# Expert weights in nine places, gathered rows turned by VectorE, and the last feed-forward closed by token halves

## What is computed

```python
# experts: 32, two for each token out of one group of 8
hid = jax.nn.silu(xb @ w_gate[e]) * (xb @ w_up[e])   # w_gate, w_up: 1024 x 256
ys = (hid @ w_down[e]) * gate                        # w_down: 256 x 1024
out = segment_sum(ys, slot_tok)                      # back to tokens, two rows each

# the end of the second block
f2 = swiglu(rms_norm(h, ffn2_pre_g), w_gate, w_up, w_down)
h = h + 0.5 * rms_norm(f2, ffn2_post_g)
```

## Time and profile before

| | us |
|---|---|
| median of 3 runs | 2992.62 (2992.49 to 2992.73) |
| the profiled execution, own time | 2994.38 |
| its span, first to last instruction | 2992.6 |
| TensorE busy with matmuls | 2944.8 |
| VectorE (DVE), ScalarE (ACT), GpSimd (POOL) busy | 1288.2, 652.6, 814.6 |

### The profile page before, as it was taken

One profiled execution on the slowest core, in us unless ns is written; L12 is line 12 of the kernel. 1 busy time (PEld: TensorE's weight loads), 2 busy tenths in 40 slices (PEclk: granted clock), 3 DMA queues, 4 the chain that ended last, 5 costly groups with the idle time before them and its releaser, 6 DMA issues.

```text
span 2992.6 us, 31855 instructions
## 1 busy us (share of the span) xinstructions
PE 2944.8 (98%) x12562; PEld 1882.5 (63%) x12562; DVE 1288.2 (43%) x2193; ACT 652.6 (22%) x1082; POOL 814.6 (27%) x621
## 2 busy tenths in 40 slices
PE   9999999999999999999999999999999999999998
PEld 7865464333468754643334588888664445888887
DVE  6734443111446435431223554442573464644442
ACT  2035313111210263231112400001212351300001
POOL 5500022222124010222221144443210102344442
PEclk9999999999999999999999999999999999999999
DMA  5211125999622101249997222222221211222220
GB/s 191 85 71 43 44 90 211 381 385 389 236 72 95 73 29 57 71 159 378 377 374 314 85 85 85 85 99 92 92 77 57 71 43 58 84 85 85 86 98 28
DMA packets 81380, 412.68 MB, mean 138 GB/s; under 512 B 25872, under 2 KB 26256, under 8 KB 34768
## 3 DMA queue, kind: packets, MB, share of 16 engines
q1 hardware_dynamic: 56608, 387.57, 34.1%
q0 software_dynamic: 24624, 23.08, 2.4%
HBM read 513.31 MB, written 31.46 MB: 182 GB/s over the span
## 4 chain that ended last, share of the span: by engine, by line
PE 93%; DVE 4%; ACT 1%; issue 1%; DMA 0%; SPq 0%; POOL 0%; DVEq 0%; ACTq 0%; POOLq 0%
PE PS L1111 38%; PE PS L1045 11%; PE PS L613 8%; PE PS L1067 6%; PE PS L598 4%; PE PS L691 4%; PE PS L571 4%; PE PS L1289 4%; PE PS L1019 1%; PE PS L846 1%; PE PS L530 1%; PE PS L786 1%; PE PS L903 1%; PE PS L912 1%; PE PS L1356 1%; PE PS L518 1%
## 5 line engine op out<-in xcount | busy, mean ns | idle before, releaser
L3105 POOL TENSOR_TENSOR ATT<-ring 128x512 f32<-128x512 f32 (+1 forms) x97 | 126.2, 1301 | 1186.7 <-PE PS L1111 630.8
L1111 PE MATMUL PS<-G,ATT 128*128 128x256 f32 x1344 | 317.8, 379 | 0.0
L1111 PE MATMUL PS<-HT,ring 128*128 128x256 f32 x1376 | 313.8, 379 | 0.8 <-DVE BIG L1518 0.8
L1111 PE MATMUL PS<-G,ring 128*128 128x256 f32 x1216 | 287.6, 379 | 0.0
L1111 PEld LDWEIGHTS PS<-HT,ring 128*128 128x128 f32 x1376 | 261.2, 190 | 39.5 <-issue 2.4
L1111 PEld LDWEIGHTS PS<-G,ATT 128*128 128x128 f32 x1344 | 255.4, 190 | 36.0 <-issue 1.2
L2827 ACT ACTIVATE TMP<-PS 128x256 f32<-128x256 f32 x91 | 35.0, 384 | 1051.7 <-PE PS L1111 934.5
L613 PE MATMUL PS<-HT,ring 128*128 128x512 f32 x576 | 263.3, 600 | 0.0
L1111 PEld LDWEIGHTS PS<-G,ring 128*128 128x128 f32 x1216 | 231.0, 190 | 31.4
L1045 PE MATMUL PS<-ring,G 128*64 128x512 f32 x1024 | 226.9, 595 | 0.6 <-ACT G L2796 0.6
L613 PEld LDWEIGHTS PS<-HT,ring 128*128 128x128 f32 x576 | 104.5, 190 | 127.4 <-issue 120.9
(11 more groups left out here) (385 smaller groups left out, 4375.7 us busy)
## 6 DMA issues: line engine op xcount, KB each, us to landing
ring<-in_stream SPq DMA_DIRECT2D x163, 1024.0 KB
ring<-in_experts_gu SPq DMA_DIRECT2D x128, 1024.0 KB
ring<-in_experts_down SPq DMA_DIRECT2D x64, 1024.0 KB
G<-expert_rows SPq DMA_DIRECT2D x8, 1024.0 KB, 6.9
h_tokens<-G POOLq DMA_DIRECT2D x2, 2048.0 KB, 7.6
XT<-in_xT SPq DMA_DIRECT2D x1, 1024.0 KB, 8.3
G<-in_pT POOLq DMA_DIRECT2D x2, 512.0 KB, 6.3
out_T<-XT SPq DMA_DIRECT2D x2, 512.0 KB, 3.7
```

What stands on the lines that cost most here:

```text
L1111: mm = pe.matmul(product(g, name), x[:, k * P:(k + 1) * P], y[:, k, :], start=first and k == 0 and name in opening, stop=last and k == h - ...
L3105: pool.tensor_tensor(a["S1"], a["A21"], a["A22"], ALU.add)\
```

## The change

**Nine places.** While the experts run, three more regions hold units: two in BIG (tiles 16 to 23) and one in ATT (tiles 7 to 10), and main blocks fill the nine in turn (`PLACE`, `Ring.experts`). SP fills the two in BIG once the attention branches are projected, the one in ATT once the output projection is done, all ahead of the stage. To make room the tail weights take 4 instead of 6 units (`TW`): the down weights land where the first half of gate and up weights lay, so POOL issues them later, after that half is used; the next gate and up weights wait for the down product. Some scratch of the router and of the rotary tables moves within ATT.

**Rows turned by VectorE.** Only blocks 0 to 5 (`FIRST_BLOCKS`) keep `turn_x` and the ACT copy. For blocks 6 to 23, POOL gathers the rows in four pieces, each of 128 rows of 256 values (`gather_squares`, L3131 in the new numbering), so arranged that the 32 x 32 squares that DVE turns in one instruction (`turned_rows`, L2062, 128 x 4 x 8 x 32) land in `XGT` as the products need them. The features are numbered otherwise for it (row p*8 + k of the weights in place of k*128 + p; the weights are laid out so on the host), and `turn_x` reads XG with a stride of eight values (32 bytes). The row numbers of the pieces come from four small products (`quad_tables`), a DVE copy ahead of the stage and one behind `hidden(0)`.

**The end by halves.** The fourth chunk of `ffn(1)` becomes a `halved_chunk` with `half_norm`, and scaling, residual and store go by token halves. In the second half TensorE and ACT add tiles 4 to 7 (`OWN_X` is 4, was 3), with 256 columns each; there are six stores in place of four, half as wide.

The core of the diff:

```diff
@@ constants and places
+PLACES = 9
+SQUARE = 32
+SQUARES = P // SQUARE
+QD = D // SQUARES
+FIRST_BLOCKS = 6
+            def experts(self):
+                order = [(self.place + i) % RING if i < RING else i for i in range(PLACES)]
+                for n in range(6 * PAIRS):
+                    p = order[n % PLACES]
+                    self.fills[p] += 1
+                    yield p, self.fills[p]
-        TW = BIGF[:, 0:12 * D].rearrange("p (s n) -> p s n", s=2)
+        TW = BIGF[:, 0:8 * D].rearrange("p (s n) -> p s n", s=2)
+        PLACE = ([ring[:, i, :] for i in range(RING)] + [BIGF[:, (16 + 4 * i) * S:(20 + 4 * i) * S] for i in range(2)]
+                 + [ATT[:, 7 * S:11 * S]])
-        OWN_X = 3
+        OWN_X = 4
@@ TensorE, expert stage
                     for k in range(KD):
-                        mm = pe.transpose(PSF[:, o + k * P:o + (k + 1) * P],
-                                          XG[:, q % 2, k * P:(k + 1) * P], IDENT)
+                        mm = pe.transpose(PSF[:, o + k * P:o + (k + 1) * P], XG[:, q % 2, k:D:KD], IDENT)
...
-                        return [TW[:, side, j * UNIT:(j + 1) * UNIT] for side in range(2)], []
+                        return [TW[:, side, j % 2 * UNIT:(j % 2 + 1) * UNIT] for side in range(2)], []
...
+                def quad_tables():
+                    pe.wait_ge(Q["tab_ready"], now.next("tab_ready"))
+                    for g in range(SQUARES):
+                        mm = pe.matmul(PS[:, 7, g * NSEQ:(g + 1) * NSEQ], QUAD_LANES[:, g * P:(g + 1) * P], RT["tab"][:, 0:NSEQ],
+                                       start=g == 0, stop=True, skip_group_check=True)
...
                 gate_up(0)
+                quad_tables()
                 gate_up(1)
...
                     turn_hidden(q - 1)
-                    if q + 1 < NSEQ:
+                    if q + 1 < FIRST_BLOCKS:
                         turn_x(q + 1)
@@ DVE, expert stage
+                def turned_rows(q):
+                    v.wait_ge(Q[f"x_gather{q % 2}"], gathered(L, q))
+                    v.wait_ge(*now.prev())
+                    v.transpose(XGT[:, q % 2, :].rearrange("p (j g x) -> p g j x", j=KD, g=SQUARES),
+                                XG[:, q % 2, :].rearrange("p (g x j) -> p g j x", j=KD, g=SQUARES))\
+                        .then_inc(Q["x_blocks"], now.inc("x_blocks"))
...
                     turned_hidden(q)
+                    if FIRST_BLOCKS <= q + 2 < NSEQ:
+                        turned_rows(q + 2)
                     if q + 1 < NSEQ:
                         hidden(q + 1)
@@ POOL, expert stage
+            def gather_squares(q):
+                c = column(q)
+                for g in range(SQUARES):
+                    i = g * NSEQ + c
+                    pool.indirect_dma_start(out=XG[:, q % 2, g * QD:(g + 1) * QD], out_offset=None, in_=HQR,
+                                            in_offset=IOA(ap=quad[:, i:i + 1], axis=0),
+                                            bounds_check=SQUARES * S - 1,
+                                            oob_is_err=False).then_inc(Q[f"x_gather{q % 2}"], 16)
...
+                        if q < FIRST_BLOCKS:
+                            pool.wait_ge(Q["x_turned"], x0 + q + 1)
+                        else:
+                            pool.wait_ge(Q["x_blocks"], b0 + q + 1 - FIRST_BLOCKS)
+                        if q + 2 == FIRST_BLOCKS:
+                            pool.wait_ge(Q["quad_rows"], now.next("quad_rows"))
+                        if q + 2 < FIRST_BLOCKS:
+                            gather(q + 2)
+                        else:
+                            gather_squares(q + 2)
+                    if 1 <= q < NSEQ and ORDER[q - 1][0] == "tail":
+                        pool.wait_ge(Q["gu_ready"], 2 * (L * NSEQ + q) - 1)
+                        tail_down(L, ORDER[q - 1][1])
...
                         if kind == "tail" and n + 1 < TAILS:
-                            tail_down(L, n + 1)
+                            pool.wait_ge(Q["dn_ready"], L * NSEQ + q - 1)
+                            tail_gate_up(L, n + 1)
@@ SP, expert stage
+                sp.wait_ge(Q["lin_ready"], at[f"branches{L}"])
+                weights(RING)
+                weights(RING + 1)
+                for n in range(RING - 1):
+                    weights(n)
+                sp.wait_ge(Q["unit_done"], at[f"out{L}_end"])
+                sp.wait_ge(Q["lin_ready"], at[f"projected{L}"])
+                weights(RING + 2)
+                weights(RING - 1)
+                for n in range(PLACES, len(units)):
+                    weights(n)
@@ TensorE and DVE, the end
-                    if f == 0 and c == 3:
+                    if c == 3:
                         halved_chunk(u0 + KF + 9, g)
...
+                    for k in range(OWN_X, KD):
+                        pe.matmul(out_sum(k), IDENT, XT[:, k, c], start=(k - OWN_X) % 2 == 0, stop=False,
+                                  skip_group_check=True)
+                    half_norm(1, 3)
...
+            first_quarters(g, last, 4)
+            while st["summed"] < KD - 2:
+                sum_square()
...
+            for k in range(KD):
+                if k == 5:
+                    second_quarters(g, last)
+                residual_half(0, "ffn2_post", k)
+            rstd_wait()
+            for k in range(OWN_X, KD):
+                v.wait_ge(*now.prev())
+                v.scalar_tensor_tensor(out=G[:, k, c], in0=G[:, k, c], scalar=gain("ffn2_post", k), in1=RSTD[:, c],
+                                       op0=ALU.mult, op1=ALU.mult)\
+                    .then_inc(Q["res_scaled"], now.inc("res_scaled"))
+            for k in range(OWN_X):
+                residual_half(1, "ffn2_post", k)
```

More of the change, by code:

```diff
@@ L1073, in down @@
                         unit_used("dn_ready", x)
-                at[f"moe{L}"] = {"x_turned": now.count("x_turned"), "x_copied": now.count("x_copied")}
+                at[f"moe{L}"] = {"x_turned": now.count("x_turned"), "x_copied": now.count("x_copied"),
+                                    "x_blocks": now.count("x_blocks")}
                 at[f"moe{L}_y"] = now.count("y_ready")
+                places = plan.experts()
                 turn_x(0)
@@ L1091, in moe @@
                 down(NSEQ - 1)
+                assert next(places, None) is None
                 pe.wait_ge(Q["y_ready"], now.next("y_ready"))
@@ L1223, in ffn @@
                         pe.wait_ge(Q["wsum_ready"], sums_of(u))
-                        last = c == 3 and q == 2
-                        for name in BY_BANK if last else LATE:
+                        for name in LATE:
                             if c == 0:
@@ L1228, in ffn @@
                             mm = multiply(g, name, u, ws[q], h, hidden_blocks(q), q == 0, q == 2)
-                            if last and name in ("P6", "P4"):
-                                mm.then_inc(Q["part_done"], now.inc("part_done"))
                         mm.then_inc(Q["unit_done"], now.inc("unit_done"))
@@ L2150, in ffn @@
                 begin_sum("tile_done")
-                for c in range(3 + f):
-                    quarter_sums(g0 + KF + c, GF[:, 2 * c * S:(2 * c + 2) * S], parts=2 * f + 2 if c == 3 else None)
+                for c in range(3):
+                    quarter_sums(g0 + KF + c, GF[:, 2 * c * S:(2 * c + 2) * S])
                     for k in (2 * c, 2 * c + 1):
@@ L3012, in _ @@
             inverse_root(D, 0)
-            ffn(1, "ffn2_post")
-            for k in range(OWN_X, KD):
-                b = k - OWN_X if k < OWN_X + 2 else 2 + k - OWN_X
-                act.wait_ge(Q["res_sum"], k - OWN_X + 1)
-                act.activation(XT[:, k, :], PS[:, b, :], ACT.Copy).then_inc(Q["xp_ready"], now.inc("xp_ready"))
+            ffn(1)
+            del st["k"]
+            edge_squares(0, "edge_tile", 3, 1)
+            half_root(0, 2)
+            edge_squares(1, "tile_done", 2 * (at["ffn1"][1] + KF + 3) + 1, 1)
+            half_root(1, 3)
+            for k in range(OWN_X, KD, 2):
+                act.wait_ge(Q["res_sum"], k - OWN_X + 2)
+                act.activation(XT[:, k:k + 2, token_half(1)],
+                               PS[:, (k - OWN_X) // 2, :].rearrange("p (a n) -> p a n", a=2), ACT.Copy)\
+                    .then_inc(Q["xp_ready"], now.inc("xp_ready"))
         @block.gpsimd
@@ L3080, in tail_down @@
                     b = 2 * n + side
[L3081 removed]
+                    pool.indirect_dma_start(out=TW[:, side, 0:UNIT], out_offset=None, in_=DOWN_ROWS,
                                             in_offset=IOA(ap=widx[:, b:b + 1], axis=0),
@@ L3237, in experts, with weights @@
                     steps += [(q, 0), (q, 1)] + ([(q - 1, 2)] if q else [])
-                for q, j in steps + [(NSEQ - 1, 2)]:
-                    kind, m = ORDER[q]
-                    if kind == "main":
-                        for side in range(2):
-                            e = 2 * m + side
```

(14 more changed lines are left out.)

119 lines of the change are left out of this document (62 added, 57 removed).

## The result

| | us |
|---|---|
| changed kernel, median of 4 runs | 3022.91 (3021.70 to 3027.32) |
| kernel before, median of 4 runs | 2992.68 (2992.49 to 2994.07) |
| ratio, 95% interval | 1.0099 (1.0087 to 1.0110) |
| span of the profiled execution, after and before | 3019.9 and 2992.6 |
| TensorE busy, after and before | 2929.8 and 2944.8 |

A forecast was written before the change was run, and what follows sets the result against it. It took TensorE and the DMA engines to be both nearly full in the expert stages. First stage -14.8, second -13.6, tables +1.0 and end -2.3 gave -29.7 us against 2992.6, thus 2963 us, range 2953 to 2978.

The forecast's parts named there:

- What POOL takes over: Expert stages: 19 issues per three blocks in place of 10, 24.9 us in a 32.5 us cycle; cost none.
- (d): Rival: POOL becomes the bound if issues exceed 1.71 us each; at 2.0 us, 3017; chance 0.06 with other mishaps.
- the stages lose their gain to waits before the fourth cycle: Sign in the expert stages of the profile after that would show the prediction wrong; no size given.
- TensorE's turns: Expert blocks 6 to 23: each removed turn saves 0.87 us, 31.3 us over 36 blocks, all on the path.
- The waits for weights: Expert stages: waits for streamed weights before `down`, put at +3 us in the first stage and +2 in the second.
- Rival (a): Expert stages: the transfers have room, so no wait for weights; -36.3 us, 2956; chance 0.25.
- The part for the packets of the pieces: Expert stages: 54 more gathers a layer add 3.6 us of DMA time a layer, 0.45 a cycle.
- DVE's turning: Expert stages: turning squares on DVE takes 1.6 us a block, hidden up to some 6 us, so costs nothing.
- rival (b): `turn_x` of blocks 0 to 5: loads with a 32-byte stride take double length, +13.4 us, 2976; chance 0.14.
- The sines and cosines: Second expert stage: two waits behind DVE grow from 2.36 to 4.1 us together, plus 1.7 us for the clock.
- The end: After the last product: 15.7 us by halves in place of 18.0, -2.3 us; bounds -4 to 0.

The follow-up runs named there:

- e5: Changed kernel with POOL issuing the tail's down weights ahead of the four gathers and its next gate and up weights ahead of the scatter: 2963.56 us.
- e4: Kernel before with only the end of `ffn(1)` by halves added: 2991.27 us.
- e9: e5 with TensorE turning the rows of all blocks, nine places kept: 2983.36 us.
- e6: Changed kernel with six weight places, and the tail weights in six units with the issue order of the kernel before: 2989.40 us.
- e1: Changed kernel without the transfers of the tail weights and the waits for them; tail blocks multiply with zeros: 2957.15 us.
- e2: Changed kernel with only the tail's next gate and up weights issued ahead of the scatter: 2991.76 us.
- e8: Changed kernel with SP holding back streamed weight loads so that at most two are in flight: 3013.99 us.

## Why the prediction was wrong, point by point

**The step that failed** is "What POOL takes over", with its end "It fits, and rows are asked for two blocks ahead. Cost: none." It counted how long POOL is busy, and that count was right: L3131 takes 1006 ns on average in the changed kernel. It did not ask when each issue can be made, and how long its transfer then has. The part on the change says that the next gate and up weights of a tail wait for the down product; no term of the sum takes that up, and no case, (d) included, has this mechanism. The distance from issue to use could be worked out from rows of before. In its cycle the new place of the issue, behind the scatter of the tail's rows, is held by the down weights:

```profile
627.93 1.01 POOL L3058 DMA_INDIRECT expert_rows<-G,ATT  x1 [9.36 <-DVE G L2019]
...
630.57 0.99 POOL L3081 DMA_INDIRECT BIG<-in_experts_down,ATT  x1 [0.30 <-issue]
```

From 630.57 to the use at 638.67 are 8.1 us, less two turns of 0.87: 6.4, which is what the changed kernel has. The landing of these transfers under load had no row there and should have been bounded. It takes up to 11.2 us. The term that was put at nothing is worth 59 us: that much the order of POOL's issues alone gives back in e5. A sign that the prediction named did come, that the stages lose their gain to waits before the fourth cycle: the first wait, at 570.27, is in the third. But it had thought of the streamed weights, and for those the changed kernel has no wait in the stages.

**TensorE's turns**: right per block (0.88 measured, 0.87 said), but "all on the path" holds only while the stream keeps up. Four runs, all with tail weights on time or nearly, set the two halves of the change against each other (all with the end by halves). "Nine places" stands for a set: the places, the tail weights in four units, and POOL's order of e5; the six-place runs have the tail's six units and the order of before.

| | six places | nine places |
|---|---|---|
| TensorE turns | 2991.3 (e4) | 2983.4 (e9) |
| VectorE turns | 2989.4 (e6) | 2963.6 (e5) |

Turning on VectorE is worth 1.9 us with six places (the spreads of e4 and e6 overlap, so it may be nothing) and 19.8 with nine; three places are worth 7.9 us with the old turns and 25.8 with the new. Together they give 27.7. Neither half has its full gain without the other, for TensorE and the stream were both nearly full, as the prediction's first paragraph said, and a sum of parts against only one of them had to be checked against the other.

**The waits for weights**: forecast +3 and +2 us. In e5 TensorE's waits over the span are 41.5 us against 40.8 before: of the old ones before `down` one is left (1.8 us for 5.5), and small ones before tails and behind DVE have come. The stream ran at 399 to 407 GB/s (e5) and 407 to 410 (e1) at a share of 1.02, above the 398 assumed. Rival (a) was nearly right on this term. The part for the packets of the pieces was too large: 54 more gathers a layer at 147 packets each are 15,876 packets, and POOL's queue has 1,728 more (26352 for 24624), so its 0.45 us a cycle were about 0.05.

**DVE's turning** takes 2.03 us, not 1.6, and stays hidden in all but one place (3.7 us):

```profile
L2062 DVE STREAM_TRANSPOSE G<-G 128x1024 f32<-128x1024 f32 x36 | 73.2, 2033 | 3.8
```

**The strided loads** (rival (b)) cost no time: `turn_x` takes 1.04 us as before. But each load did become longer. This is its row in the changed kernel (min/median/max ns):

```profile
L1050 PEld LDWEIGHTS PS<-MATS,G x96: 185/188/209, 485.9 to 1390.3; 128*128 128x128 f32 x96
```

It had 138/140/143, and has that in e4 too, where the rows are read without a stride. The loads of the eight products overlap, and 0.05 us more on each does not show in their 1.04 us. The prediction's bound of 13.4 us went wrong there: it put every load on the path. By the rule on lines of 16 bytes that it named beside (b) (the Trainium skill, SBUF — State Buffer, "Door 1: The DMA port swizzle"), a stride of eight f32 is not free. The trace agrees on the load, by 0.05 us, and not on the time of the kernel. DVE's 2.03 us can't tell, for there is no transpose without a stride to hold it against.

**The sines and cosines**: the changed kernel has no wait of this kind. Its two waits of 1.75 us behind DVE stand at the ends of the two stages, where the kernel before had 1.75 and 2.10. In e5, where TensorE is early, the two are 2.08 and 1.55 us, 3.6 together, and behind the first `down` took 5.35 us for 3.65. The forecast was 4.1 with 1.7 for the clock, so it was close.

**The end**: from the last product (3005.51 + 1.46 = 3006.97) to 3019.9 are 12.9 us, 14.2 with the 1.3 us of `half_norm` ahead of it, against 18.0 before and 15.7 in the forecast. DVE's last instruction:

```profile
3016.93 0.42 DVE L1489 TENSOR_TENSOR XT<-XT,G 128x256 f32<-128x256 f32 x1
```

ends at 3017.35, so the last store takes 2.55 us where the forecast took over 4.1 from before.

In sum: e5, which has every part of the change with the tail weights on time, came to 2963.56, where the forecast said 2963.0. Such closeness is partly luck, since the turns gave 22.5 us net and not 31.3, and the missing waits and the end made up for part of it. What the forecast priced was near; what it left out was twice as large.

## What to carry to other kernels

Where a change makes a transfer share its destination with another, follow the issue, not the issuing engine's busy time: note what releases it, what stands ahead of it in its queue, when its data are needed, and hold that distance against the longest landing under load. Two nearly full resources must be relieved together, and an edit priced against one of them is worth little alone (1.9 us of 31 here). And when a wait on the critical path is removed, look at once for the next late transfer behind it: e2 recovered half, and three lines moved beside it the rest.

## What the runs showed of the hardware

- The indirect transfers of the tail weights landed in 2.1 us at the best and 11.2 us in the full stage, though all 64 moved 0.03 MB together (e1). The 2.1 us are those of the last tail (issue at 1625.74), when the DMA engines had little to carry (3 GB/s from 1626 to 1632 us). The Trainium skill (DMA: Bandwidth & Descriptors, "Anatomy of one DMA — SWDGE (gpsimd) path") gives 2.0 us plus the bytes over 436 GB/s for a DMA that GpSimd issues. The trace agrees with the first number where the engines are idle, and is 9 us from it where they are full. What makes the 9 us is not shown. Where TensorE waited for such a transfer with two loads in flight (e8), it was used 4.7 to 7.7 us after its second issue.
- With two loads of 1 MB in flight the stream had 345 to 370 GB/s in three stretches of 40 us (e8), with nine places and no such limit 399 to 407.
- In the changed kernel the granted clock fell behind each wait of 3.5 to 4.9 us, and the tail's `gate_up` took 8.6 to 10.0 us for 7.09; behind 2.77 us (at 1503.98) it took 7.09. The length of the wait alone does not decide. `down`, normally 3.65 us, took 5.35 behind 2.08 us in e5, as behind 2.10 before, and 3.65 behind 2.06 in e1 (at 1429.67), behind 2.78 in e2 (at 619.81) and behind 3.90 in e8 (at 712.06).
- A weight load of 128 x 128 f32 values for a transpose took 0.14 us, and 0.19 with a stride of 32 bytes on what it reads; beside the products this cost nothing.
- A transpose by DVE of 128 x 1024 f32 values in squares of 32, with a stride of 32 bytes on its input, takes 2.03 us.
